# Backward columns in the 512-column products, and a 32-byte gap behind each feature tile of xa

## The chip, the cores and the metric

The kernel runs on one core of a Trainium2 chip. Its time is the device time of one execution in microseconds: 2200.41 us as the median of two runs (2200.11 and 2200.72). All data is float32 at the kernel's edges.

## What is computed

Two blocks follow each other on a sequence of 256 tokens with 2048 features. The first is gated linear attention, a SwiGLU layer and a gated embedding, the second an mLSTM with a pooling branch. Cut to the products with weights, which are nearly all of the work:

```python
proj = einsum('btd,de->bte', rmsnorm(x), gla_w_in)       # q, k, v, og, lr
h = x + einsum('bte,ed->btd', attention(q, k, v, lr) * silu(og), gla_w_out)
h = h + swiglu(rmsnorm(h), ffn_w_in, ffn_w_out)          # 2048 -> 2 x 5632 -> 2048
h = rmsnorm(h + sigmoid(rmsnorm(h) @ ple_w_gate) * (p @ ple_w_proj))
...
proj = rmsnorm(h) @ w_in                                 # q, k, v, o_g, z_a, gates, u_b, z_b, g_a, g_b
br_a = mlstm(...) @ w_proj_mlstm
br_b = (pool(u_b) @ pool_w * pool_scale * silu(z_b)) @ w_proj_pool
out  = (sigmoid(g_a) * br_a + sigmoid(g_b) * br_b) @ w_out
y    = h + rmsnorm(out)
```

The weights come from HBM once, 410 MB in all. Each product needs float32 accuracy, which the kernel gets from float32r products, one pass each, by splitting both operands.

## The kernel before

**The split.** A weight or a feature value is written as hi + lo, both float32r. The product is then hi x hi + hi x lo + lo x hi, so each tile of weights is multiplied three times.

**The tiling.** The program is a list of jobs (`plan`), one for each weight matrix or part of it. A job has column tiles of 512 output features, and each of these has granules: two tiles of 128 input features by 512 columns, 1024 columns wide in SBUF. For each granule SyncE loads the raw weights into one of 8 slots (`raw`), ScalarE copies them as float32r into one of 4 slots of `w_hi` (line 801), VectorE subtracts to get `w_lo` (line 1686), and TensorE multiplies. Semaphores count granules: `landed`, `hi_ready`, `lo_ready`, and `consumed`, with which TensorE gives the slot back.

**The products.** In `product` (lines 1314 to 1316) the stationary operand of 128 x 128 is a piece of the features, turned so that the input feature lies on the partitions, and the moving operand is 512 columns of the weights. For each of a granule's two feature tiles and each of the two halves of the tokens there are three products into the same PSUM bank `a[t]`: `xh` with `hi`, `xh` with `lo`, `xl` with `hi`. A granule has 12 products. Each has a weight load of its own (LDWEIGHTS, the rows of PEld), which runs beside the product ahead of it.

**Other products.** The first four granules use `opening_product` (lines 1341, 1346, 1349), in runs of two or four with the same part. Narrow products (lines 1304 to 1307) have the weights stationary and the features moving. The pool products (1269 to 1271) move 256 columns, those of the embedding (1291 to 1293) and of the attention's output (1507 to 1509) 512. The scores (1494, 1535) are plain float32.

**Where the features lie.** Four buffers hold features as tiles of 256 tokens, 1024 bytes each: `xa_hi`/`xa_lo` and `xb_hi`/`xb_lo` with 16 tiles, `hid_hi`/`hid_lo` with 24, `yb_hi`/`yb_lo` with 8. Blocks take turns between xa and xb. The buffers from `raw` to `xb_lo` follow each other with sizes that are multiples of 512 bytes, and lines such as `o += (w_hi_at - o) % NC` move hid, yb and the attention's `A_hi` up until they have the same remainder by 512 as `w_hi`. A moving operand starts at a multiple of 2048 bytes in `w_hi` or `w_lo`, a stationary one at a multiple of 512 in its buffer. So in all the products of lines 1314 to 1316 the two operands begin at the same place within 512 bytes.

**Who writes xa.** ScalarE writes the hi part, VectorE the lo part, most often one tile of 256 columns at a time; in one job (`pm`) two tiles at once, as 128x512 (lines 826 and 1911). While xa is not needed as features, `PPJ`, the embedding's product, lies on it.

Of the kernel before, what the change touches and what calls it, by code (L numbers as in the profile page):

```python
# [5 lines left out]
F32 = mybir.dt.float32  # L6
F32R = mybir.dt.float32r
# [6 lines left out]
P = 128  # L14
T = 256
# [4 lines left out]
NC = 512  # L20
RAW_SLOTS = 8
HL_SLOTS = 4
LAG = 3
PP_AT = 8

# [90 lines left out]
def build(nc, x, p, mixer_norm, gla_w_in, gla_w_gate_up, gla_b_gate, gla_out_norm, gla_w_out,  # L116
# [31 lines left out]
    with ctx:  # L148
# [4 lines left out]
        def at(name, shape, dt, offset):  # L153
            return nc.alloc_sbuf_tensor_at(name, shape, dt, offset=offset)

        def own(name, shape, dt, size):
            offset = used_to[0]
            used_to[0] += (size + 31) // 32 * 32
            return at(name, shape, dt, offset), offset

        raw, _ = own("raw", [P, RAW_SLOTS, 2 * NC], F32, RAW_SLOTS * 4096)
        w_hi, w_hi_at = own("w_hi", [P, HL_SLOTS, 2 * NC], F32R, HL_SLOTS * 4096)
        w_lo, _ = own("w_lo", [P, HL_SLOTS, 2 * NC], F32R, HL_SLOTS * 4096)
        xa_hi, xa_at = own("xa_hi", [P, 16, T], F32R, 16384)
        xa_lo, _ = own("xa_lo", [P, 16, T], F32R, 16384)
        xb_hi, xb_at = own("xb_hi", [P, 16, T], F32R, 16384)
        xb_lo, _ = own("xb_lo", [P, 16, T], F32R, 16384)
        H, h_at = own("H", [P, 2, D], F32, 16384)
        ident, _ = own("ident", [P, P], F32, 512)
        vec, _ = own("vec", [P, VEC_ROWS], F32, 4 * VEC_ROWS)  # L170
        cbias, _ = own("cbias", [P, 32], F32, 128)
        cw, _ = own("cw", [P, P], F32, 512)
        ssq, _ = own("ssq", [P, 6, 2, 4], F32, 192)
        msq, _ = own("msq", [P, 8, 2], F32, 64)
        rstd, _ = own("rstd", [P, 8, 2], F32, 64)
        S2 = 6
        half, _ = own("half", [P, 16], F32, 64)
        hss, _ = own("hss", [P, 16], F32, 64)
        hms, _ = own("hms", [P, 16], F32, 64)
        hrs, _ = own("hrs", [P, 16], F32, 64)  # L180
        fold, _ = own("fold", [4 * RANK, 3 * RANK], F32, 192)
        junk, _ = own("junk", [P, NC], BF16, 1024)
# [39 lines left out]
        pT_hi = at("pT_hi", [P, 2, T], F32R, hid_at + 20 * 1024)  # L222
        pT_lo = at("pT_lo", [P, 2, T], F32R, hid_at + 24576 + 20 * 1024)
        pT_raw = at("pT_raw", [P, 2, T], F32, hid_at + 20 * 1024 + 2048)
        PPJ = at("PPJ", [P, 4, 2, NC], F32, xa_at)
        fn_bc = at("fn_bc", [P, D], F32, hid_at + 24576)

        o = phase
# [104 lines left out]
        def gran(job, n, j):  # L333

            return job.g0 + n * job.G + j
# [48 lines left out]
        def token_halves_apart(job, n, j):  # L384

            return job.name == "out" and isinstance(n, int) and n == job.n - 1 and j >= job.G - HL_SLOTS

# [844 lines left out]
        def _(pe):  # L1232
            def product(job, n, j, ns, only=None):

                g = gran(job, n, j)
                k0, kc = job.gr[j]
                hl = (job.g0 + ns * job.G + j) % HL_SLOTS
                w = job.w
                a = acc_of(job, ns)
                if j == 0 and not (isinstance(n, int) and job.t0 + n < 2):  # L1240
                    for t in range(2):
                        pe.wait_ge(evac[t], E(job, n) - 2)
                if ns == 0:
                    for r, b in needs(job, j):
                        pe.wait_ge(tp_read[b], r + 1)
                    by_tile = {"wo": "y", "f1": "wo", "pg": "f2o", "ub": "pg", "out": "pm"}.get(job.name)
                    if by_tile and j // 2 < BY_VECTOR[by_tile]:
                        pe.wait_ge(tile_low, turned_count(by_tile, j // 2) + 1)
                    if by_tile in SHARED and j == 7:
                        pe.wait_ge(half_low, SHARED.index(by_tile) + 1)  # L1250
                    if job.name == "pm":
                        pe.wait_ge(tile_low, turned_count("ya", 4))
                    if job.name == "f1o":
                        pe.wait_ge(hid_ready, hid_tile("f1", j) + 1)
                    if job.name == "f2o" and not is_pp(job, j):
                        pe.wait_ge(hid_ready, hid_tile("f2", j - (j > PP_AT)) + 1)
                pe.wait_ge(lo_ready, g + 1)
                if job.name == "pool":
                    if j == 2:
                        for t in range(2):  # L1260
                            pe.wait_ge(pp_read[t], 4)
                    to = pool_bank(j)
                    for t in range(2):
                        for kk in range(kc):
                            hi = w_hi[:, hl, kk * w:(kk + 1) * w]
                            lo = w_lo[:, hl, kk * w:(kk + 1) * w]
                            xh = xt_part(job, 0, k0 + kk)[:, t * P:(t + 1) * P]
                            xl = xt_part(job, 1, k0 + kk)[:, t * P:(t + 1) * P]
                            nc.tensor.matmul(to[:, t * w:(t + 1) * w], xh, hi, start=(kk == 0), stop=False)
                            nc.tensor.matmul(to[:, t * w:(t + 1) * w], xh, lo, start=False, stop=False)  # L1270
                            ins = nc.tensor.matmul(to[:, t * w:(t + 1) * w], xl, hi, start=False, stop=(kk == kc - 1))
                    ins.then_inc(consumed, 1)
                    return
                if job is JOBS[0]:
                    pe.wait_ge(x_split, min(max(j, 1), 8))
                to = mx[0] if is_lr(job, j) else a[0]
                for kk in range(kc):
                    k = k0 + kk
                    hi = w_hi[:, hl, kk * w:(kk + 1) * w]
                    lo = w_lo[:, hl, kk * w:(kk + 1) * w]  # L1280
                    first = j == 0 and kk == 0
                    last = j == (8 if job is JOBS[0] else job.G - 1) and kk == kc - 1
                    if is_pp(job, j):
                        if k == 0 and n:
                            for t in range(2):
                                pe.wait_ge(pp_read[t], n)
                        if k == 0 and n == 0:
                            pe.wait_ge(p_low, 1)
                        for t in range(2):
                            xh, xl = pT_hi[:, k, t * P:(t + 1) * P], pT_lo[:, k, t * P:(t + 1) * P]  # L1290
                            nc.tensor.matmul(mx[t][:, :], xh, hi, start=(k == 0), stop=False)  # L1291
                            nc.tensor.matmul(mx[t][:, :], xh, lo, start=False, stop=False)  # L1292
                            ins = nc.tensor.matmul(mx[t][:, :], xl, hi, start=False, stop=(k == 1))  # L1293
                        if k == 1:
                            ins.then_inc(consumed, 1)
                        continue
                    if narrow(job, j):

                        w = narrow(job, j)
                        first, last = kk == 0, kk == kc - 1  # L1300
                        xh, xl = xt_part(job, 0, k), xt_part(job, 1, k)
                        both = w_hi[:, hl, 2 * kk * w:(2 * kk + 2) * w]
                        if first:
                            nc.tensor.matmul(to[0:2 * w, 0:T], both, xh, start=True, stop=False)
                        ins = nc.tensor.matmul(to[0:w, 0:T], both[:, 0:w], xl, start=False, stop=False)
                        if not first:
                            ins = nc.tensor.matmul(to[0:2 * w, 0:T], both, xh, start=False, stop=last)
                        if kk == kc - 1:
                            ins.then_inc(consumed, 1)
                        continue  # L1310
                    for t in range(2) if only is None else (only,):
                        xh = xt_part(job, 0, k)[:, t * P:(t + 1) * P]
                        xl = xt_part(job, 1, k)[:, t * P:(t + 1) * P]
                        nc.tensor.matmul(a[t][:, 0:w], xh, hi, start=first, stop=False)  # L1314
                        nc.tensor.matmul(a[t][:, 0:w], xh, lo, start=False, stop=False)  # L1315
                        ins = nc.tensor.matmul(a[t][:, 0:w], xl, hi, start=False, stop=last)  # L1316
                    if kk == kc - 1 and only != 0:
                        ins.then_inc(consumed, 1)
                    elif last and only == 0:
                        ins.then_inc(half_done, 1)  # L1320
# [1212 lines left out]
```

## Time and profile before

| what | value |
|---|---|
| median of two runs | 2200.41 us |
| profiled execution | 2200.2 us |
| its span, first to last instruction | 2198.5 us |
| TensorE busy | 2188.7 us |
| VectorE busy | 1574.8 us |
| ScalarE busy | 1082.1 us |
| mean granted TensorE clock | 1.000 of 2.4 GHz |
| read from HBM | 410 MB, 188 GB/s |

The times of the table come from one profiled execution. A product's row is longer than the distance to the next one's start, because products are pipelined; the distance between starts tells what a product costs. The rows are in the section below.

### The profile page before, as it was taken

The page shows a single profiled execution, that of the slowest core. Times are in us where ns is not written, and L with a number is a line of the kernel's source. Part 1 is how long each engine was busy: PE and PEld are TensorE (multiplying, and loading weights), DVE is VectorE, ACT ScalarE, POOL GpSimd, SP SyncE. Part 2 cuts the span into 40 slices and gives each one's busy share as a digit, 9 for nine tenths or more (in the row PEclk, how much of TensorE's full clock was granted, in tenths as well). Part 3 has the DMA queues.
Part 4 walks back from the last instruction along what each step waited for, and adds up shares of the span by engine and source line. Part 5 has one row for each costly group of instructions (what it writes and reads, how often), then busy time and mean ns, then how long its engine had stood idle before and what let it go on. Part 6 is the DMA issues. An engine that isn't in the chain of part 4 may idle for free.

```text
span 2198.5 us, 27733 instructions
## 1 busy us (share of the span) xinstructions
PE 2188.7 (100%) x9954; PEld 1819.9 (83%) x9954; DVE 1574.8 (72%) x2395; ACT 1082.1 (49%) x1369; POOL 19.8 (1%) x41
## 2 busy tenths in 40 slices
PE   9999999999999999999999999999999999999998
PEld 8888888888888888888888888888888888888887
DVE  6887888877776457777778846889455559645875
ACT  5564554544444334444446545555445555443443
POOL 0000000000000000000000000000000000000000
PEclk9999999999999999999999999999999999999999
DMA  9654566666666666666666656666665556666663
GB/s 281 182 163 122 179 196 189 200 192 195 194 193 192 192 195 191 196 191 194 186 217 198 200 152 191 183 199 181 201 176 171 171 162 205 196 195 211 191 192 114
DMA packets 282925, 413.96 MB, mean 188 GB/s; under 512 B 21071, under 2 KB 145883, under 8 KB 282299
## 3 DMA queue, kind: packets, MB, share of 16 engines
q1 hardware_dynamic: 281806, 408.55, 61.9%
q10 hardware_dynamic: 1008, 3.94, 0.5%
q8 instruction: 68, 1.11, 0.2%
q14 instruction: 43, 0.35, 0.0%
HBM read 410.33 MB, written 2.10 MB: 188 GB/s over the span
## 4 chain that ended last, share of the span: by engine, by line
PE 99%; issue 0%; DMA 0%; DVE 0%; ACT 0%; DVEq 0%; POOLq 0%; POOL 0%; SPq 0%; ACTq 0%
PE acc L1314 31%; PE acc L1316 31%; PE acc L1315 31%; PE mx L1494 1%; PE mx L1535 0%; PE tp L1362 0%; DMA H<-in_x 0%; PE tp L1508 0%; PE tp L1507 0%; PE tp L1509 0%; PE mx L1291 0%; PE mx L1293 0%; PE mx L1292 0%; PE mx L1472 0%; PE tp L1552 0%
## 5 line engine op out<-in xcount | busy, mean ns | idle before, releaser
L1686 DVE TENSOR_TENSOR w_lo<-raw,w_hi 128x1024 fp32r<-128x1024 f32 (+1 forms) x769 | 934.9, 1219 | 524.5 <-ACT w_hi L801 520.7
L801 ACT CAST w_hi<-raw 128x1024 fp32r<-128x1024 f32 (+1 forms) x769 | 803.0, 1046 | 913.9 <-PE acc L1316 897.0
L1314 PE MATMUL acc<-w_hi,xa_hi 128*128 128x512 f32 x2228 | 874.8, 393 | 0.0
L1316 PE MATMUL acc<-w_hi,xa_lo 128*128 128x512 f32 x2228 | 867.4, 389 | 0.0
L1315 PE MATMUL acc<-w_lo,xa_hi 128*128 128x512 f32 x2228 | 867.2, 389 | 0.0
L1316 PEld LDWEIGHTS acc<-w_hi,xa_lo 128*128 128x128 f32 x2228 | 418.2, 188 | 87.8
L1314 PEld LDWEIGHTS acc<-w_hi,xa_hi 128*128 128x128 f32 x2228 | 418.5, 188 | 84.8
L1315 PEld LDWEIGHTS acc<-w_lo,xa_hi 128*128 128x128 f32 x2228 | 418.6, 188 | 84.2
L1314 PE MATMUL acc<-w_hi,xb_hi 128*128 128x512 f32 x384 | 149.6, 390 | 0.0
L1316 PE MATMUL acc<-w_hi,xb_lo 128*128 128x512 f32 x384 | 149.4, 389 | 0.0
L1315 PE MATMUL acc<-w_lo,xb_hi 128*128 128x512 f32 x384 | 149.4, 389 | 0.0
L1314 PE MATMUL acc<-w_hi,hid_hi 128*128 128x512 f32 x352 | 136.9, 389 | 0.0
L1315 PE MATMUL acc<-w_lo,hid_hi 128*128 128x512 f32 x352 | 136.9, 389 | 0.0
L1316 PE MATMUL acc<-w_hi,hid_lo 128*128 128x512 f32 x352 | 136.9, 389 | 0.0
L1941 DVE STREAM_TRANSPOSE stage<-stage 32x128 f32<-32x128 f32 x352 | 106.6, 303 | 8.0
L1856 DVE STREAM_TRANSPOSE stage<-H 32x256 f32<-32x256 f32 x192 | 83.7, 436 | 3.3
L1316 PEld LDWEIGHTS acc<-w_hi,xb_lo 128*128 128x128 f32 x384 | 72.1, 188 | 15.1
L1315 PEld LDWEIGHTS acc<-w_lo,xb_hi 128*128 128x128 f32 x384 | 72.1, 188 | 14.9
L1314 PEld LDWEIGHTS acc<-w_hi,xb_hi 128*128 128x128 f32 x384 | 72.1, 188 | 14.8
L1315 PEld LDWEIGHTS acc<-w_lo,hid_hi 128*128 128x128 f32 x352 | 66.1, 188 | 13.8
L1314 PEld LDWEIGHTS acc<-w_hi,hid_hi 128*128 128x128 f32 x352 | 66.1, 188 | 13.7
L1316 PEld LDWEIGHTS acc<-w_hi,hid_lo 128*128 128x128 f32 x352 | 66.1, 188 | 13.6
(313 smaller groups left out, 1240.4 us busy)
## 6 DMA issues: line engine op xcount, KB each, us to landing
raw<-in_w_in SPq DMA_DIRECT2D x192, 512.0 KB, 3.8
raw<-in_ffn_w_in SPq DMA_DIRECT2D x352, 256.0 KB, 2.9
raw<-in_gla_w_in SPq DMA_DIRECT2D x95, 512.0 KB, 4.0
raw<-in_ffn_w_out SPq DMA_DIRECT2D x88, 512.0 KB, 3.7
raw<-in_w_in SPq DMA_DIRECT2D x128, 256.0 KB, 3.0
raw<-in_gla_w_out SPq DMA_DIRECT2D x32, 512.0 KB, 4.1
raw<-in_ple_w_gate SPq DMA_DIRECT2D x32, 512.0 KB, 4.0
raw<-in_w_proj_mlstm SPq DMA_DIRECT2D x32, 512.0 KB, 3.7
```

The costliest lines, as they stand in the source:

```text
L801: nc.scalar.copy(w_hi[:, hl, 0:kc * job.w], raw[:, slot, 0:kc * job.w]).then_inc(hi_ready, 1)
L1314: nc.tensor.matmul(a[t][:, 0:w], xh, hi, start=first, stop=False)
L1315: nc.tensor.matmul(a[t][:, 0:w], xh, lo, start=False, stop=False)
L1316: ins = nc.tensor.matmul(a[t][:, 0:w], xl, hi, start=False, stop=last)
L1494: ins = nc.tensor.matmul(score_columns(to, t, i), key, query, start=(c == 0), stop=(c == 1))
L1686: nc.vector.tensor_tensor(w_lo[:, hl, 0:kc * job.w], raw[:, slot, 0:kc * job.w], w_hi[:, hl, 0:kc * job.w].bitcast(F32), ALU.subtract) \
L1856: ins = nc.vector.transpose(tokens[32 * b:32 * b + 32], columns[own])
L1941: ins = nc.vector.transpose(turned_blocks(a)[32 * b:32 * b + 32], hidden_blocks(b)[own])
```

## The change

Three things are edited. The 512-column products of `product` get both their moving operand and their output with the order of the columns turned round, so that column 511 is read and written first. The two xa buffers get rows of 264 elements per feature tile in place of 256, of which the first 256 are used; `PPJ`, which lies on them, gets the same pitch. The scratch area of the program for dynamic DMAs is set to 8192 bytes, which makes the room for the wider rows and moves all buffers down.

```diff
+X_ROW = T + 8
...
-        xa_hi, xa_at = own("xa_hi", [P, 16, T], F32R, 16384)
-        xa_lo, _ = own("xa_lo", [P, 16, T], F32R, 16384)
+        xa_rows_hi, xa_at = own("xa_hi", [P, 16, X_ROW], F32R, 16 * 4 * X_ROW)
+        xa_rows_lo, _ = own("xa_lo", [P, 16, X_ROW], F32R, 16 * 4 * X_ROW)
+        xa_hi, xa_lo = xa_rows_hi[:, :, 0:T], xa_rows_lo[:, :, 0:T]
...
-        PPJ = at("PPJ", [P, 4, 2, NC], F32, xa_at)
+        PPJ = at("PPJ", [P, 4, 4 * X_ROW], F32, xa_at)[:, :, 0:2 * NC].rearrange("p n (t c) -> p n t c", t=2)
...
-                        nc.tensor.matmul(a[t][:, 0:w], xh, hi, start=first, stop=False)
-                        nc.tensor.matmul(a[t][:, 0:w], xh, lo, start=False, stop=False)
-                        ins = nc.tensor.matmul(a[t][:, 0:w], xl, hi, start=False, stop=last)
+                        to = a[t][:, 0:w][:, ::-1]
+                        nc.tensor.matmul(to, xh, hi[:, ::-1], start=first, stop=False)
+                        nc.tensor.matmul(to, xh, lo[:, ::-1], start=False, stop=False)
+                        ins = nc.tensor.matmul(to, xl, hi[:, ::-1], start=False, stop=last)
...
-    nc = bacc.Bacc("TRN2", target_bir_lowering=False, num_devices=1)
+    nc = bacc.Bacc("TRN2", target_bir_lowering=False, num_devices=1, dynamic_dma_scratch_size=8192)
```

The order of the instructions on every engine is the same as before. The only rows that differ are the copies and subtractions of lines 826 and 1911, which go over xa in the shape 128x2x256 in place of 128x512.

## Rows read from the trace of the kernel before

**Rows 1.** The page: busy us and share of the span; tenths in 40 slices.
```profile
PE 2188.7 (100%) x9954; PEld 1819.9 (83%) x9954; DVE 1574.8 (72%) x2395; ACT 1082.1 (49%) x1369; POOL 19.8 (1%) x41
...
PEclk9999999999999999999999999999999999999999
```
**Rows 2.** Waits of TensorE: us in total, times, longest us.
```profile
PE tp L1611 <- POOL stage L732: 1.1, 1, 1.1
PE acc L1622 <- DMA H<-in_x: 1.0, 1, 1.0
PE acc L1341 <- ACT w_hi L801: 0.5, 1, 0.5
```
**Rows 3.** Groups by form: count | busy us, mean ns of one | idle before.
```profile
L1316 PE MATMUL acc<-w_hi,xa_lo 128*128 128x512 f32 x2228 | 867.4, 389 | 0.0
...
L1316 PE MATMUL acc<-w_hi,xb_lo 128*128 128x512 f32 x384 | 149.4, 389 | 0.0
...
L1316 PE MATMUL acc<-w_hi,hid_lo 128*128 128x512 f32 x352 | 136.9, 389 | 0.0
...
L1316 PE MATMUL acc<-w_hi,yb_lo 128*128 128x512 f32 x64 | 24.9, 389 | 0.0
```
**Rows 4.** Stretches: us, busy us and instructions by engine, granted clock, DMA share, GB/s.
```profile
500.00:700.00 200.00, 200.00 (x884) 165.62 (x883) 146.60 (x245) 89.09 (x100) 0.00 (x0) 1.00 0.64 194
700.00:900.00 200.00, 200.00 (x884) 165.58 (x884) 120.76 (x164) 82.56 (x85) 0.00 (x0) 1.00 0.63 192
900.00:1100.00 200.00, 200.00 (x884) 165.62 (x883) 147.91 (x237) 91.16 (x108) 0.00 (x0) 1.00 0.64 192
```
**Rows 5.** Line 1316 with xa: weight loads and products, ns min/median/max.
```profile
L1316 PEld LDWEIGHTS acc<-w_hi,xa_lo x2228: 187/188/192, 18.4 to 2190.6; 128*128 128x128 f32 x186
L1316 PE MATMUL acc<-w_hi,xa_lo x2228: 387/389/398, 18.6 to 2190.8; 128*128 128x512 f32 x186
```
**Rows 6.** The chain that ended last, in the opening: start us, us.
```profile
11.91 0.94 PE acc L1341 x4
12.85 0.92 PE acc L1346 x4
...
16.97 0.91 PE acc L1349 x4
```
**Rows 7.** The same chain at the scores of the second block.
```profile
1605.43 0.65 PE mx L1535 x3
```
**Rows 8.** Timeline at 1357 us: start us, us, instruction.
```profile
1357.59 0.39 PE L1316 MATMUL acc<-w_hi,xa_lo 128*128 128x512 f32 x1
1357.60 0.31 PEld L1562 LDWEIGHTS tp<-ident,gi 128*8 128x8 f32 x2
...
1357.82 0.38 PE L1562 MATMUL tp<-ident,gi 128*8 128x128 f32 x2
```
**Rows 9.** Groups by form: the writers of two xa tiles at once.
```profile
L1911 DVE TENSOR_TENSOR xa_lo<-gates,xa_hi 128x512 fp32r<-128x512 f32 x6 | 3.9, 684 | 0.0
...
L826 ACT CAST xa_hi<-gates 128x512 fp32r<-128x512 f32 x6 | 3.4, 616 | 0.0
```
**Rows 10.** The page: DMA queues, kind: packets, MB, share of 16 engines.
```profile
q1 hardware_dynamic: 281806, 408.55, 61.9%
q10 hardware_dynamic: 1008, 3.94, 0.5%
q8 instruction: 68, 1.11, 0.2%
q14 instruction: 43, 0.35, 0.0%
```
**Rows 11.** Stretches, columns as in rows 4: the one fullest for VectorE.
```profile
250.00:400.00 150.00, 150.00 (x677) 124.52 (x676) 128.56 (x203) 77.54 (x106) 0.70 (x1) 1.00 0.65 202
```
**Rows 12.** Waits of ScalarE, columns as in rows 2.
```profile
ACT w_hi L801 <- PE acc L1316: 897.0, 623, 2.6
```

## The prediction

> **What bounds the kernel now.** I read the page from the top: busy times and the granted clock, then the costliest groups, then the waits of TensorE, then stretches of the middle of the run, and last single products beside their weight loads. The busy line shows TensorE at 2188.7 of 2198.5 us, with the granted clock at 9 tenths or more (the digit's ceiling) in every slice, so it stands at the 2.4 GHz level throughout [rows 1]. All waits of TensorE together are 2.6 us and lie in the first microseconds [rows 2]. So only the time between the starts of two products matters; VectorE and ScalarE can lose or gain without moving the end.
>
> The products that the change touches are lines 1314 to 1316, all of 128x512. Their three lines carry 2228 products each with xa, 384 with xb, 352 with hid and 64 with yb [rows 3]: 3028 x 3 = 9084. Three stretches of 200 us hold nothing else. In each, 884 products overlap the stretch; a product's row is 0.389 us long and one that began just before the stretch counts too, so the distance between starts is (200 + 0.389) / 884 = 226.7 ns [rows 4]. 9084 x 226.7 ns = 2059 us, 94% of the span. At the granted clock 512 columns need 512 / 2.4 = 213.3 ns. So 13.4 ns of each product, 122 us in all, is something else, and that is all that this change can win.
>
> **What the 13.4 ns are.** The rows tell two things. First, they are no constant of the array. The same instruction, line 1316 with xa, lasts 387, 389 or up to 398 ns, while its weight load stays at 187 to 192 [rows 5]. In the opening, runs of four last 0.94, 0.92 and 0.91 us, that is 235 down to 228 ns each, for the same shape and the same kind of operands [rows 6]. Something outside the multiplication stretches a product by varying amounts, and in the long stretches it has settled at 226.7. Second, where two clocks are spent on each column, nearly nothing is lost: three products of 128x256 at line 1535 take 0.65 us, 217 ns for 512 clocks, each with a weight load of the same 128x128 beside it [rows 7]. What differs is that the float32r products ask for a new moving element in every clock. My reading, which no row proves, is that the moving stream and the weight load of the next product read SBUF at the same time and get into each other's way, the more so the faster the stream. Then the order in which addresses are read, and the distance between the two operands' addresses, set the loss. These are the two things that the change alters.
>
> Against this reading stands one row. At 1357.59 us a product runs beside a load of only 8 columns, and the next start still comes 0.23 us later [rows 8]. If the loss were made by the load, it should have shrunk there. The product behind it has another data type, though, and its start may carry a cost of its own.
>
> **The change, part by part.**
> - *Order of the columns.* Every one of the 9084 products reads its 512 columns from the last to the first and writes PSUM in the same order. No instruction is added, removed or moved on any engine, and the products, their sums and who waits for them stay. Its price per product is not shown by any row, since no product of before reads backward. From below it is bounded by the clock: 213.3 ns, -13.4. The nearest row without the loss is line 1535 with 217 ns, -9.7. From above the nearest rows are the opening's runs, 235 ns, +8.3.
> - *Gaps in xa.* Tile k of xa begins 32 k bytes later within 512 bytes than the moving columns, where before all began alike. 2228 x 3 = 6684 products are concerned; the other 2400 keep their old distance, since 16 x 1056 bytes is again a multiple of 512. This cost lies in the same bounds, 213.3 to 235 ns, and acts on the same wait, so I price both edits together.
> - *Writers of xa.* The six copies of 128x512 into xa_hi and the six subtractions into xa_lo (0.62 and 0.68 us each [rows 9]) now write two pieces of 256 with a gap between. Were they half as long again, that is at most 12 x 0.35 = 4 us on engines that are not the bound. They lie beside TensorE's work: nothing.
> - *Transfers and scratch.* The smaller scratch area moves every buffer 8192 bytes down. No queue but hardware ones and instruction fetch appears, so nothing uses that area [rows 10]: nothing.
> - *PPJ, the narrow products, the pool products, the opening, the heads.* Not reversed; of them only those that read xa see the gaps, 12 x 3 in the opening and some sixty narrow ones. At 8 ns each that is under 1 us either way.
>
> Taken together I choose 217 ns, the row that is nearest to a product whose reads are not disturbed. Two streams that run the same way from the same offset can stay side by side for long; two that run toward each other meet and part. 9084 x (226.7 - 217) = 88 us less.
>
> **What comes late next.** With products at 217 ns a granule of twelve takes 2.60 instead of 2.72 us. VectorE is fullest in 250 to 400 us, 128.6 of 150 us [rows 11]; the stretch would be 143.6 us long, and VectorE 90% busy in it. Its splits mostly wait for ScalarE's, which wait for TensorE to free a buffer: 897 us of ScalarE's idle time ends with line 1316 [rows 12]. So there is room. The transfers' share of 0.64 in the middle [rows 4] would become 0.67. No new bound appears.
>
> **Sum.** 2198.5 us of span lie in a profiled execution of 2200.2 us, against a median of 2200.4, so they agree. 2200.2 - 88 = **2112 us**. Its own range goes from the clock's floor, 2200.2 - 122 = 2078, to 2156, where it stops being a gain of over 2%.
>
> A page of the Trainium skill gives the same floor in another way. "TensorE: Matmul & The Clock Gate", in Part 1, has back-to-back products of 512 columns at 215.7 ns; this trace has 226.7 for its float32r ones, so the rule does not hold for them as they stand. By 215.7 the estimate would be 100 us less, 2100 us.
>
> **Rivals.**
> 1. *The loss does not come from the order of reading*, and stays 226.7. For it: the row with the 8-column load [rows 8], and that products with xa, xb, hid and yb all read 389 ns [rows 3]. Against: all four have the same offset between their operands, so their agreement says nothing on offsets; and the loss does vary [rows 5, 6]. The same result would come if the reversal were undone before the chip reads the columns. Time: 2200, with 2165 to 2225 around it for a small effect either way. Chance 0.32.
> 2. *The new pattern settles at a worse distance* (slower). Place: the products with xa, where the start of the stationary tile now takes 16 different distances from the moving one, so that the even rhythm that holds for hundreds of products now is broken at each tile. Price: the opening's 235 ns, 6684 x 8.3 = 55 us, 2256; if all products go there, 9084 x 8.3 = 75 us, 2276. It decides from 44 us on, that is 6.6 ns on each product with xa. For it: products have been seen at 235 in this very kernel [rows 6]. Against: these stand right behind breaks and settle again. Chance 0.15.
> 3. *Writing PSUM backward runs at half rate.* Each product would take two clocks for a column, as line 1535 does now [rows 7], 512 x 2 / 2.4 = 427 ns: 9084 x 200 ns = 1817 us more, about 4017 us. No row writes PSUM backward, so nothing in the trace speaks for it or against it. Chance 0.08.
>
> The rule behind the third is in the Trainium skill, "PSUM — Partial Sum Buffer", Specifications: PSUM has cachelines of 8 bytes, and any access pattern that is not contiguous slows matmuls a lot. No row of this case shows it. Whether a reversed run still fills both words of a line in turn is what it would hang on. And "SBUF — State Buffer", Who interferes with whom, says that TensorE never waits on anyone and reads moving and stationary operands through two independent ports; by that the first rival is right and the time is 2200. The varying 387 to 398 ns [rows 5] sit badly with it.
>
> **Numbers.** Forecast 0.45, no effect 0.32, slower by distance 0.15, slower by half rate 0.08. The range goes from 2085, just above the floor, to 2280, over the second rival's upper end; it leaves out the third rival (0.08) and a few hundredths below. The likeliest case alone has 2078 to 2156. A gain of over 2%, 44 us, is about what a measurement of this kernel can tell with ease from no change: faster 0.45, within 2% 0.33 (the first rival and a little of the second), slower 0.22.
>
> **What would show it.** In the middle stretches, where 884 products overlap 200 us, the changed kernel should have (200 + 0.38) / 0.217 = 923; 884 means the first rival, under 866 the second, about 470 the third. The count in stretches with xb and hid against those with xa parts the two edits: a gain with xa only would come from the gaps, one everywhere from the direction. The rows of line 1316 should be shorter by the same 10 ns than 389 or should at least be even; the weight loads should stay at 188. PE should remain at 100% and the waits of TensorE near 3 us. I am wrong if TensorE gets waits for w_lo, or if the distance stays at 226.7.

## The result and the profile after

The changed kernel takes **2259.98 us** (median of two runs, 2259.41 and 2260.55) against 2200.41: a ratio of 1.0268, with a 95% interval of 1.0243 to 1.0293. It is slower by 60 us, where 88 us less were forecast. The profiled execution took 2260.55 us, 2258.8 of them the span. In it the products are lines 1317 to 1319.

From the page of the changed kernel, with the columns of [rows 1]:
```profile
PE 2249.4 (100%) x9954; PEld 1824.3 (81%) x9954; DVE 1576.8 (70%) x2395; ACT 1079.6 (48%) x1369; POOL 19.8 (1%) x41
...
PEclk9999999999999999999999999999999999999999
```
TensorE is still the whole span, at the same granted clock. Its waits, with the columns of [rows 2]:
```profile
PE tp L1614 <- POOL stage L734: 1.1, 1, 1.1
PE tp L1436 <- DVE gates L2290: 0.9, 1, 0.9
PE acc L1625 <- DMA H<-in_x: 0.2, 1, 0.2
```
None for `w_lo` has come in, and all together are 2.2 us, where they were 2.6. So the 60 us lie in the distance between the starts of products. The same three stretches as in [rows 4]:
```profile
500.00:700.00 200.00, 200.00 (x859) 161.13 (x858) 142.76 (x240) 86.09 (x99) 0.00 (x0) 1.00 0.61 188
700.00:900.00 200.00, 200.00 (x858) 161.13 (x858) 114.98 (x152) 78.78 (x81) 0.00 (x0) 1.00 0.63 188
900.00:1100.00 200.00, 200.00 (x859) 161.17 (x858) 143.46 (x237) 86.11 (x100) 0.00 (x0) 1.00 0.61 186
```
859 products overlap 200 us where 884 did; the third stretch also holds 24 of the embedding's products, which have 512 columns too and are not reversed. From the first, (200 + 0.397) / 859 = **233.3 ns** from start to start, 6.6 more than before. 9084 x 6.6 = 60 us, the whole difference. One line's instructions, which answer to [rows 5] and, with xb, hid and yb, to [rows 3]:
```profile
L1319 PEld LDWEIGHTS acc<-w_hi,xa_lo x2228: 187/188/188, 19.2 to 2250.9; 128*128 128x128 f32 x186
L1319 PE MATMUL acc<-w_hi,xa_lo x2228: 395/397/403, 19.4 to 2251.2; 128*128 128x512 f32 x186
...
L1319 PE MATMUL acc<-w_hi,xb_lo x384: 397/397/400, 334.9 to 2161.1; 128*128 128x512 f32 x192
...
L1319 PE MATMUL acc<-w_hi,hid_lo x352: 395/397/398, 694.2 to 1174.9; 128*128 128x512 f32 x176
...
L1319 PE MATMUL acc<-w_hi,yb_lo x64: 397/397/398, 2027.4 to 2071.5; 128*128 128x512 f32 x64
```
Every product has become 8 ns longer, with xb, hid and yb as with xa. Only xa got gaps, so the gaps can't be the cause; the reversal is what all four share. The weight loads are unchanged at 188.

ScalarE waits a little longer for TensorE to free a buffer, with the columns of [rows 12]:
```profile
ACT w_hi L803 <- PE acc L1319: 969.5, 632, 2.6
```

### The profile page after: what moved, and what is told of

It reads as the page before. It is cut to its first block, busy times and chain, and to the rows that moved or that the text cites. A ratio compares the mean times of both kernels' runs of the same rounds, so it can differ in the third digit from the quotient of the medians.

```text
span 2258.8 us, 27733 instructions
## 1 busy us (share of the span) xinstructions
PE 2249.4 (100%) x9954; PEld 1824.3 (81%) x9954; DVE 1576.8 (70%) x2395; ACT 1079.6 (48%) x1369; POOL 19.8 (1%) x41
## 4 chain that ended last, share of the span: by engine, by line
PE 98%; DMA 1%; issue 0%; DVE 0%; SPq 0%; ACT 0%; DVEq 0%; POOLq 0%; POOL 0%; ACTq 0%
PE acc L1317 31%; PE acc L1318 31%; PE acc L1319 31%; PE mx L1497 1%; PE mx L1538 0%; PE tp L1365 0%; DMA raw<-in_gla_w_in 0%; DMA H<-in_x 0%; PE tp L1511 0%; PE mx L1294 0%; PE mx L1293 0%; PE tp L1512 0%; PE tp L1510 0%; PE mx L1295 0%; PE mx L1475 0%
## 5 line engine op out<-in xcount | busy, mean ns | idle before, releaser
L1317 PE MATMUL acc<-w_hi,xa_hi 128*128 128x512 f32 x2228 | 892.1, 400 | 0.0
L1319 PE MATMUL acc<-w_hi,xa_lo 128*128 128x512 f32 x2228 | 885.1, 397 | 0.0
L1318 PE MATMUL acc<-w_lo,xa_hi 128*128 128x512 f32 x2228 | 885.0, 397 | 0.0
```

Source lines behind the costliest of these rows:

```text
L1317: nc.tensor.matmul(to, xh, hi[:, ::-1], start=first, stop=False)
L1318: nc.tensor.matmul(to, xh, lo[:, ::-1], start=False, stop=False)
L1319: ins = nc.tensor.matmul(to, xl, hi[:, ::-1], start=False, stop=last)
```

## The experiments

All are told against the kernel before. Where a diff shows one operand, the other products of `product` are edited alike. e1, e2, e8 and the changed kernel compute what the kernel before does. In e13 part of one product is missing, and in all others the columns land in the wrong order or the same operand is used over and over, so those runs stand for time alone. The distance between starts is worked out from the stretch of 500 to 700 us as above or, where it is called a mean over the run, from all pairs of neighbouring products in the trace. Where the distances vary from tile to tile the two can be apart by up to 1 ns. Times of e1 and e2 are medians of four runs, all others are single runs; before had 2200.35 to 2202.21 us beside them.

**e1_reverse_only.** The reversal without the gaps and without the smaller scratch area.
```diff
+to = a[t][:, 0:w][:, ::-1]
-nc.tensor.matmul(a[t][:, 0:w], xh, hi, start=first, stop=False)
+nc.tensor.matmul(to, xh, hi[:, ::-1], start=first, stop=False)
```


> Only the columns are reversed, in reading and writing; xa keeps its rows of 256 and the scratch area its old size. Theory A (the direction makes the whole loss: distance between starts 233.3 ns instead of 226.7 in all 9084 products, +61 us): about 2260 us, and products with xa at 233.3 without the pairs of 236 and 231 that two tiles show in the changed kernel. Theory B (the gaps make it): 2200 us. Theory C (both are needed): something between.

Measured: 2258.65 us against 2200.35, ratio 1.0264 (1.0247 to 1.0281). Its stretches:
```profile
500.00:700.00 200.00, 200.00 (x858) 161.13 (x858) 142.71 (x241) 86.48 (x99) 0.00 (x0) 1.00 0.61 187
700.00:900.00 200.00, 200.00 (x859) 161.12 (x858) 114.99 (x150) 78.10 (x80) 0.00 (x0) 1.00 0.63 189
```
The same 233.3 ns. The intervals of its ratio and of the changed kernel's lie over each other: the reversal alone is enough for the whole loss.

**e2_gaps_only.** The gaps and the smaller scratch area, the products forward.
```diff
-xa_hi, xa_at = own("xa_hi", [P, 16, T], F32R, 16384)
+xa_rows_hi, xa_at = own("xa_hi", [P, 16, X_ROW], F32R, 16 * 4 * X_ROW)
+xa_hi, xa_lo = xa_rows_hi[:, :, 0:T], xa_rows_lo[:, :, 0:T]
```


> Only the gaps behind the tiles of xa and the smaller scratch area; columns run forward. Theory A: 2200 us, 226.7 ns for all products. Theory B: the products with xa (6684) are slower, those with xb, hid and yb stay at 226.7; by 6.7 ns that would be +45 us, 2245. If the distance of the two operands matters at all, the sixteen feature tiles should differ from each other.

Measured: 2237.74 us, ratio 1.0169 (1.0152 to 1.0186). Line 1318 is its third product:
```profile
L1318 PE MATMUL acc<-w_hi,xa_lo x2228: 388/394/404, 18.6 to 2228.3; 128*128 128x512 f32 x186
...
L1318 PE MATMUL acc<-w_hi,xb_lo x384: 389/389/397, 332.0 to 2138.6; 128*128 128x512 f32 x192
...
L1318 PE MATMUL acc<-w_hi,hid_lo x352: 389/389/395, 688.0 to 1160.9; 128*128 128x512 f32 x176
```
Here the two edits part. xb and hid keep the 389 of before, while xa reads 394 in the middle. By feature tile and half of the tokens the mean distance with xa lies between 229.0 and 235.5 ns, and the pattern repeats after 8 tiles, which is 256 bytes of gaps. Over the run the mean with xa is 232.6, where before it was 227.0, and 6684 products by some 5.6 ns are 37 us. The moving stream of this run is that of the kernel before. All buffers lie 8192 bytes lower, which xb and hid don't feel; with xa only the place that the weight loads read from has changed within 512 bytes. So that place has a say in the distance when the stream runs forward. Where the products change from hid to xa, at 818.13 us, the first five distances with xa, all with tile 0, are 227, 226, 227, 227 and 226 ns; the sixth, beside the load of tile 1, is 235. The gaps thus cost when the stream runs forward, and in the changed kernel they cost nothing measurable on top: 2259.98 against 2258.65.

**e3_read_backward** and **e4_write_backward.** One half of the reversal each. 
```diff
# e3: SBUF backward, PSUM forward
+nc.tensor.matmul(a[t][:, 0:w], xh, hi[:, ::-1], start=first, stop=False)
# e4: SBUF forward, PSUM backward
+nc.tensor.matmul(a[t][:, 0:w][:, ::-1], xh, hi, start=first, stop=False)
```


> The moving operand is read backward, PSUM is written forward, so each product's columns land in the wrong order; the work is the same. Theory A1 (reading SBUF backward costs the 6.7 ns): 233.3 ns and 2260 us. Theory A2 (writing PSUM backward costs them): 226.7 ns and 2200 us.

> The moving operand is read forward, PSUM is written backward, so each product's columns land in the wrong order. Theory A1 (the read): 226.7 ns, 2200 us. Theory A2 (the write): 233.3 ns, 2260 us. If each costs a part, e3 and e4 lie between and add up to 60 us.

Measured: 2258.57 and 2200.72 us. One stretch of e3, then the same of e4:
```profile
500.00:700.00 200.00, 200.00 (x859) 161.15 (x858) 142.72 (x239) 85.64 (x98) 0.00 (x0) 1.00 0.62 187
```
```profile
500.00:700.00 200.00, 200.00 (x884) 165.68 (x883) 146.58 (x245) 89.41 (x101) 0.00 (x0) 1.00 0.64 193
```
The loss is in the order in which SBUF is read. Writing PSUM backward costs nothing here.

**e5_load_one_column** and **e6_load_one_column_back.** Each weight load reads one column 128 times, so that it stays at one address; the moving stream goes forward in e5 and backward in e6.
```diff
-nc.tensor.matmul(a[t][:, 0:w], xh, hi, start=first, stop=False)
+nc.tensor.matmul(a[t][:, 0:w], xh[:, 0:1].broadcast_to([P, P]), hi, start=first, stop=False)
# e6: hi[:, ::-1]
```


> Columns forward. The stationary operand of every 512-column product is its first column, repeated 128 times, so a weight load fetches one address 128 times; all tokens of a half get one result. Theory L (the loss is a collision of the moving stream with the addresses that the next load reads): the distance falls from 226.7 toward 213 to 217 ns, up to 120 us less, 2080 to 2115 us. Theory M (the loss comes with the moving stream alone, whatever the load reads): 226.7 ns, 2200 us.

> The same with the moving operand read backward (PSUM written forward). Theory L: the order of reading matters only against a load that walks through addresses, so this run is as e5. Theory M: 233.3 ns as in e3, 2259 us.

Measured: 2238.09 and 2258.07 us. The third product of e5:
```profile
L1316 PEld LDWEIGHTS acc<-w_hi,xa_lo x2228: 187/188/193, 18.9 to 2228.5; 128*128 128x128 f32 x186
L1316 PE MATMUL acc<-w_hi,xa_lo x2228: 387/396/403, 19.1 to 2228.7; 128*128 128x512 f32 x186
```
A stretch of e6:
```profile
500.00:700.00 200.00, 200.00 (x859) 161.18 (x858) 142.76 (x240) 85.70 (x98) 0.00 (x0) 1.00 0.61 188
```
Forward the distance rises to 231.7 ns ((200 + 0.39) / 865; the mean over the run is 231.0), with nearly all single ones between 224 and 234; backward it stays at 233.3. A load that no longer walks takes nothing off the loss, forward or backward. Forward it even adds 4 ns, which again shows that what the load reads matters to a forward stream.

**e7_move_one_column.** The mirror image: the moving stream stays at one address, the load is whole.
```diff
+nc.tensor.matmul(a[t][:, 0:w], xh, hi[:, 0:1].broadcast_to([P, NC]), start=first, stop=False)
```


> Every 512-column product has its first moving column repeated 512 times, so the moving stream stays on one address; the load walks as before. Theory L in a form with banks: the stream meets the load only while this passes the one bank, so the distance falls below 226.7. Theory M, with the loss in stepping from one address to the next: 213 to 217 ns, 2080 to 2115 us. A loss that has nothing to do with SBUF addresses: 226.7, 2200 us.

Measured: 2112.98 us. Its third product:
```profile
L1316 PEld LDWEIGHTS acc<-w_hi,xa_lo x2228: 187/189/190, 19.6 to 2103.4; 128*128 128x128 f32 x186
L1316 PE MATMUL acc<-w_hi,xa_lo x2228: 377/379/380, 19.9 to 2103.6; 128*128 128x512 f32 x186
```
The distances are 215 and 216 ns, and 220 in half of the pairs from the first to the second product. The mean is (200 + 0.379) / 926 = 216.4, so 10 ns of the 13.4 above the clock's floor vanish while every weight load still takes its 188 ns. So the loss needs a moving stream that walks. Whether it needs the load too this run can't tell: both theories of the expectation, the one of a meeting in banks too, allowed a shorter distance here.

**e8_shift_64_128_192_32.** Forward; xa, xb, hid and yb begin 64, 128, 192 and 32 bytes away from where the moving columns begin within 512 bytes.
```diff
+used_to[0] += 64          # ahead of xa and of xb
-hid_at = phase + (w_hi_at - phase) % NC
+hid_at = phase + (w_hi_at - phase) % NC + 192
-o += (w_hi_at - o) % NC   # yb
+o += (w_hi_at - o) % NC + 32
+nc = bacc.Bacc(..., dynamic_dma_scratch_size=8192)
```


> Columns forward, tiles of 1024 bytes without gaps, but each buffer lies at a distance of its own from the weights within 512 bytes: xa 64, xb 128, hid 192, yb 32 bytes. In e2 the tiles of xa took between 229.0 and 235.5 ns, with a pattern that repeats after eight tiles, 256 bytes. Theory D (the distance of the two operands decides): four different values for the four buffers, constant within each, and one of them may be under 226.7. Theory N (only the change of the distance from tile to tile disturbs): 226.7 for all, 2200 us.

Measured: 2254.93 us. The third product with each buffer:
```profile
L1318 PE MATMUL acc<-w_hi,xa_lo x2228: 388/394/405, 18.5 to 2245.6; 128*128 128x512 f32 x186
...
L1318 PE MATMUL acc<-w_hi,xb_lo x384: 390/393/404, 333.0 to 2155.6; 128*128 128x512 f32 x192
...
L1318 PE MATMUL acc<-w_hi,hid_lo x352: 394/397/398, 692.0 to 1170.5; 128*128 128x512 f32 x176
...
L1318 PE MATMUL acc<-w_hi,yb_lo x64: 392/395/396, 2022.2 to 2066.3; 128*128 128x512 f32 x64
```
The mean distances over the run are 233.3, 232.4, 231.3 and 233.3 ns. None of the four shifts is better than none, and all are worse than 226.7.

**e9_groups_back, e10_within_back.** The reversal in two grains: groups of four columns (16 bytes) from last to first with each read forward, and groups forward with each read backward.
```diff
# e9
+nc.tensor.matmul(a[t][:, 0:w], xh, hi.rearrange("p (b c) -> p b c", c=4)[:, ::-1, :], start=first, stop=False)
# e10
+nc.tensor.matmul(a[t][:, 0:w], xh, hi.rearrange("p (b c) -> p b c", c=4)[:, :, ::-1], start=first, stop=False)
```


> The moving columns are read in groups of four (16 bytes): the groups from the last to the first, the four columns of a group forward. PSUM is written forward, so the columns land in the wrong order. Theory G (the order of the 16-byte groups costs the 6.7 ns of e3): 233.3 ns, 2259 us. Theory I (the order within a group costs them, each column fetched against its neighbour): 226.7 ns, 2200 us.

> The groups of four run forward, the four columns of a group backward; wrong order in PSUM again. Theory G: 226.7 ns, 2200 us. Theory I: 233.3 ns, 2259 us.

Measured: 2258.75 and 2200.23 us. The third product of e9, then that of e10:
```profile
L1316 PE MATMUL acc<-w_hi,xa_lo x2228: 395/397/400, 18.8 to 2249.4; 128*128 128x512 f32 x186
```
```profile
L1316 PE MATMUL acc<-w_hi,xa_lo x2228: 387/389/398, 18.6 to 2190.9; 128*128 128x512 f32 x186
```
The order of the 16-byte groups carries all of the loss, the order inside them none.

**e11_one_group, e12_256_bytes, e17_one_32, e18_one_64.** The stream goes round in a small piece: 16, 256, 32 and 64 bytes.
```diff
# e11; e12: 64 columns, 8 times; e17: 8 columns, 64 times; e18: 16 columns, 32 times
+nc.tensor.matmul(a[t][:, 0:w], xh, hi[:, 0:4].unsqueeze(1).broadcast_to([P, NC // 4, 4]), start=first, stop=False)
```


> The first four moving columns (16 bytes) are repeated 128 times. e7, with one column, had 215 to 220 ns. If the loss comes with each step to a new group of 16 bytes: 215 to 220 as in e7, 2113 us. If it comes with each step to a new element: 226.7 or more, 2200 us and above.

> The first 64 moving columns (256 bytes) are repeated 8 times. If the loss is made by walking through places that repeat every 256 bytes, as the pattern of eight tiles in e2 suggests, this is no different from walking through 2048 bytes: 226.7 ns, 2200 us. If it needs the whole 2048 bytes (longer walk, no return): between 215 and 226.7.

> Products move the first 8 columns (32 bytes, two 16-byte groups) of the tile 64 times over, forward; the sums are thus not those of the reference. Known: one group over and over gives 215.4 ns between starts (2112 us), 256 bytes over and over 226.7 (2201 us). Theory A, every step to another 16-byte group costs the same: 226.7 ns already here, 2201 us, 884 products in 200 us. Theory B, the loss comes from something that a walk meets only over a longer stretch: 215 to 221 ns, 2112 to 2155 us, 905 products or more. A value above 226.7 would say that the step back, every second one here, is dearer than the step forward: with 63 steps back and 64 forward, halfway between forward and backward gives 230 ns, 2231 us.

> Products move the first 16 columns (64 bytes, four 16-byte groups) of the tile 32 times over, forward; the sums are thus not those of the reference. Theory A, every step to another 16-byte group costs the same: 226.7 ns, 2201 us. Theory B, a longer walk is needed: between the time with 32 bytes and that with 256 bytes (2201 us). If the step back to the first group is what is dear, this run lies nearer to 226.7 than the one with 32 bytes: every fourth step is one back, so a quarter of the way to backward, 228.4 ns, 2216 us.

Measured: 2111.8, 2200.71, 2112.29 and 2332.91 us. The first stretch of e17, then of e18:
```profile
500.00:700.00 200.00, 200.00 (x926) 174.31 (x925) 145.38 (x232) 91.34 (x101) 0.00 (x0) 1.00 0.67 203
```
```profile
500.00:700.00 200.00, 200.00 (x829) 156.84 (x828) 137.97 (x232) 82.98 (x95) 0.00 (x0) 1.00 0.59 181
```

| piece gone round | products in 500 to 700 us | distance, ns |
|---|---|---|
| one column (e7) | 926 | 215 to 220 |
| 16 bytes (e11) | 927 | 215 to 220 |
| 32 bytes (e17) | 926 | 215 to 220 |
| 64 bytes (e18) | 829 | 232 to 246, mean 241.7 |
| 256 bytes (e12) | 884 | 226.7 |
| 2048 bytes, forward (before) | 884 | 226.7 |

Neither theory held in both runs. Two groups in turn cost nothing, though every fourth column steps to the other group: a step between 16-byte groups is not dear in itself. Four groups cost more than 16 or 128 do, so the loss doesn't grow with the length of the walk either, and a share of the backward loss for each step back, 2216 us for e18, is far from 2333. The mean of e18 over the run is 241.5.

**e13_short_load, e14_short_load_back.** The second product of each three has a stationary operand of 32 columns; e13 reads forward, e14 backward.
```diff
-nc.tensor.matmul(a[t][:, 0:w], xh, lo, start=False, stop=False)
+nc.tensor.matmul(a[t][0:32, 0:w], xh[:, 0:32], lo, start=False, stop=False)
```


> Columns forward. The middle one of each three products (xh with lo, line 1315) uses 32 stationary columns in place of 128, so that its weight load, which runs beside the product of line 1314, is a quarter as long; the sums lack part of xh x lo. Theory L (the loss comes from the load that runs beside a product): the distance from line 1314 to line 1315 falls by most of its 11 ns, the two others stay near 226.7; about -25 us. Theory M (the moving stream alone loses it): all three near 226.7, or, if the stationary width of the product itself counts, the one from 1315 to 1316 falls.

> As e13, with the moving operand read backward. Theory L: the distance from 1314 to 1315 falls by most of its 18 ns, to 216 to 220. Theory M: 233.3 for all, 2259 us.

Measured: 2238.4 and 2259.82 us. The second product of e13 with its load:
```profile
L1315 PEld LDWEIGHTS acc<-w_lo,xa_hi x2228: 107/108/113, 18.2 to 2228.6; 128*32 128x32 f32 x186
L1315 PE MATMUL acc<-w_lo,xa_hi x2228: 386/396/404, 18.4 to 2228.8; 128*32 128x512 f32 x186
```
and a stretch of e14:
```profile
500.00:700.00 200.00, 200.00 (x859) 138.27 (x858) 142.76 (x241) 86.67 (x99) 0.00 (x0) 1.00 0.61 187
```
The first product of each three runs beside a load of 108 ns in place of 188. Its distance should have shrunk if the length of the load made the loss. In e13 its mean is 229.4 ns over the run, more than 226.7 and not less; the two others have 233.0 and 230.9. In e14 it is 233.4, like all others. Backward, the load's length has no effect that shows. No run leaves the load out altogether.

**e15_every_second_group, e16_two_halves.** Longer steps forward: groups 0, 2, 4 and so on, then 1, 3, 5; and groups in turn from the first and the second half, 1024 bytes apart.
```diff
# e15
+nc.tensor.matmul(a[t][:, 0:w], xh, hi.rearrange("p (b e c) -> p e b c", e=2, c=4), start=first, stop=False)
# e16
+nc.tensor.matmul(a[t][:, 0:w], xh, hi.rearrange("p (h b c) -> p b h c", h=2, c=4), start=first, stop=False)
```


> The moving columns are read in groups of four (16 bytes): groups 0, 2, 4 ... 126, then 1, 3, 5 ... 127, so each step is 32 bytes forward; wrong order in PSUM. If a backward step costs more than a forward one because the stream relies on finding the next 16 bytes ready: 233 ns or more. If only the direction against something else that moves forward counts: at most 233, perhaps under 226.7.

> Groups of four columns alternately from the first and the second half of the 512: steps of +1024 and -1008 bytes; both groups of a pair lie at the same place within 256 bytes. If each step out of order costs, this is the worst: over 233 ns. If only the place within 256 bytes counts, half of the steps change nothing and the distance falls toward 221.

Measured: 2245.32 and 2410.31 us. A stretch of e16, the slowest order found:
```profile
500.00:700.00 200.00, 200.00 (x801) 151.58 (x801) 135.43 (x231) 84.07 (x91) 0.00 (x0) 1.00 0.57 176
```
e15 has 867 in the stretch, 231.1 ns, with single distances from 228 to 235; over the run its mean is 231.9. e16 has (200 + 0.413) / 801 = 250.2 ns, most of them near two values, 246 and 254. So backward is not the only order that is worse than forward, nor the worst.

## Why the prediction was wrong

**What bounds the kernel, and what can be won: right.** TensorE alone sets the end, 9084 products times their distance gives the time, and 13.4 ns of each are no constant of the array. e7, e11 and e17 took 10 of them away and reached 2112 us, where 9084 x 10.3 = 94 us less would be 2107; TensorE's waits have grown by some 3 us there. The 215.7 ns that the prediction cited from the Trainium skill, "TensorE: Matmul & The Clock Gate", Part 1, are met by the 215 and 216 of these three runs and by no float32r product with 512 different columns. The count in 200 us was the right thing to look at: 859 told the result in one row.

**The step that failed** is "two that run toward each other meet and part", by which 217 ns were taken for the reversed products. The runs put something else in its place. Reading the groups of 16 bytes of the moving operand from last to first makes the distance 233.3 (e3, e9), and it stays there when the load stands on one column (e6) and when the load beside a product takes 108 ns in place of 188 (e14). So it isn't a meeting with the load that sets the backward distance, no parting of two streams gave anything back, and the reversal swapped a good order for a worse one.

**The reading under it,** that "the moving stream and the weight load of the next product read SBUF at the same time and get into each other's way", fails as the account of the 13.4 ns, though not in every part. Against it: the loss does not shrink when the load stands on one column (e5) or is little over half as long (e13), and it nearly goes with whole loads once the moving stream stays within 32 bytes (e7, e11, e17). For it: with the moving stream left as it was, another place of the stationary tiles (e2, e8), a load on one column (e5) or a shorter one (e13) moves the mean distance of a forward stream from 226.7 to between 229 and 235. And in the kernel before, all 346 distances of 229 to 240 ns stand within twelve products behind work of another kind, with operands that begin alike as in the long stretches of 226.7. So the load has a part in the forward distance; that taking it away would give the 13.4 ns back is not shown, since no run is without loads.

**The choice of the bound.** The distance that was measured, 233.3, lay inside the bounds of the prediction, near the upper one of 235 that came from the opening [rows 6]. I chose 217, near the lower one, because line 1535 [rows 7] seemed the nearest row. It is near in its loads only; its stream asks for a new element half as often, and nothing in the trace showed such a stream and one that reads backward to be alike.

**The row that spoke against it was the better guide.** At 1357 us a product beside a load of 8 columns was followed 0.23 us later [rows 8]. I set it aside for the other data type of the product behind it. e13, where the product behind has the same type, says what that row said: 229.4 ns beside the short load.

**The gaps: priced together with the reversal, which hid that they act apart.** Alone and forward they cost 37 us (e2). This is the price of the second rival, 55 us, with 5.6 ns in place of 8.3. Under a backward stream the distance is 233.3 with the gaps (changed kernel) and without (e1), so there they are worth nothing. The mechanism of the interplay isn't shown; what is shown is that a forward stream over 256 bytes or more had 226.7 only where both operands begin alike (before, e4, e10, e12), and means of 229 to 235 with every other tile position, load or length tried (e2, e5, e8, e13), while the backward one is at 233.3 in all of them (e1, e3, e6, e9, e14).

**The rivals.** The second, slower by a worse distance, gave 2256 to 2276 us and a count under 866, and so the time and the sign; but it put the cause at the changed distances of the xa products, with all products only as its upper price. In the changed kernel xa and xb don't part. Its size was right by luck, its place wrong, and no rival held that reading backward is itself dearer. The first, no effect, is out by the two traces. The third, PSUM at half rate, is refuted by e4: 2200.72 us. The rule behind it, in the Trainium skill, "PSUM — Partial Sum Buffer", Specifications, counts any pattern that is not contiguous as slow; if a run of columns from last to first is meant by that, the measurement differs: it is not slow here.

**Priced at nothing, and rightly:** the writers of xa over two pieces, 0.62 and 0.68 us in both kernels:
```profile
L1914 DVE TENSOR_TENSOR xa_lo<-gates,xa_hi 128x512 fp32r<-128x512 f32 x6 | 3.9, 685 | 0.0
...
L828 ACT CAST xa_hi<-gates 128x512 fp32r<-128x512 f32 x6 | 3.4, 615 | 0.0
```
Also the scratch area (e1 and e3 leave it as it was) and VectorE's room, which e17 shows for the fast case too: at 2112 us TensorE's waits for `w_lo` come to 2.7 us in all, its longest 1.1.
```profile
PE acc L1314 <- DVE w_lo L1686: 2.7, 5, 1.1
```

**What stays open.** Why a walk costs what it does. The orders give 215 to 220 (16 and 32 bytes round), 226.7 (forward), 231.9 (every second group), 233.3 (backward), 241.5 (64 bytes round) and 250 ns (two halves in turn) over the run, and no single rule that I formed fits all six. One regularity is in the steadiest rows. With hid in the kernel before the mean is 226.67 ns, with hid in the changed one 233.35, and all 191 distances with yb in e18 are 240. At 2.4 GHz these are 544, 560 and 576 clocks, 32, 48 and 64 more than the 512 columns. What stands behind these steps of 16 no run shows. The Trainium skill, "SBUF — State Buffer", Specifications, says that SBUF has lines of 16 bytes, that two hits to a line are needed for full bandwidth, and that each cross to a new one pays. The size of the group agrees: order within 16 bytes is free (e10). The rest does not fit: a forward walk hits each line four times and still takes 226.7 ns, and 32 bytes round cross as often as it does and have none of its 10 ns of loss (e17). The same page, Who interferes with whom, has it that TensorE waits on no one. No run here shows another engine in its way. Its own two streams are another matter: the place of the stationary tiles alone moved the mean distance with xa from 227.0 to 232.6 ns (e2). No version faster than the kernel before came out: the three runs at 2112 us multiply the same few columns over and over.

## What to carry to other kernels

Leave the moving operand of float32r products of 128x512 in ascending order of addresses, and begin the stationary and the moving operand at the same place within 512 bytes; giving up the first alone cost this kernel 58 us (2.6%, e1), giving up the second 37 us with xa (1.7%, e2) and 55 us with all four buffers (2.5%, e8). Writing PSUM from last to first cost nothing, nor did turning round the order inside 16 bytes of the moving operand. When a loss per instruction is put down to the meeting of two streams, hold or shorten the one that is said to be in the way and see if the loss goes: e5 is that run, and it would have spoken against this prediction's reading before any of its numbers were used. Holding the other one (e7) doesn't decide, as a meeting needs both.

## What the runs showed of the hardware

- A float32r product of 128x512 starts 226.7 ns after the one before it with aligned operands read forward, 233.3 read backward, and 215 to 220 when its moving columns lie within 32 bytes; granted clock 1.00 throughout.
- Four 16-byte groups in turn are dearer (241.7 ns in the stretch) than sixteen (226.7) and than two (215 to 220).
- Groups taken in turn from two places 1024 bytes apart cost 250 ns from start to start, the most seen.
- A backward stream is insensitive: gaps, a load on one column and a load of 32 columns all leave it at 233.3. A forward stream reacts to each of them, by 2 to 9 ns in the mean.
- The median span of a weight load is 188 to 190 ns for 128 columns in all orders, and 108 for 32 columns.
